# Hymba-style encoder layer: first transposes, recurrent gates, sigmoids and gelus in a new order in the two projection stages

## The chip, the cores and the metric

One NeuronCore of a Trainium2 chip runs one launch of the whole layer. The metric is device time in microseconds, the median of the runs. The engines are TensorE (PE), VectorE (DVE), ScalarE (ACT), GpSimd (POOL) and SyncE (SP, which here only issues DMAs).

## The reference, cut to what matters

The layer takes x of 4096 frames x 1024 and computes, in float32:

```
u = RMSNorm(x)
[q|k|v|x_lru|g_lru] = u @ w_in                       # 5 x 512 columns
out_A = stick-breaking attention(q, k, v)            # 8 heads x 64
xc = causal depthwise conv(4)(x_lru)
r = sigmoid(xc @ w_rgate + b_r); i = sigmoid(xc @ w_igate + b_i)   # 8 blocks x 64
a = exp(8 r log_sigmoid(lam)); u' = sqrt(1 - a^2) * i * xc
h_t = a_t h_(t-1) + u'_t                             # along the frames
out_B = h * gelu(g_lru)
h = x + concat(RMSNorm(out_A), RMSNorm(out_B)) @ w_out
h = h + HierMoE(RMSNorm(h)); y = RMSNorm(h)
```

The change touches only the projections and the recurrent branch, which are the first quarter of the time.

## The kernel before, in words

The stages run one after the other with a barrier between them: qkv, lru, attention, mix, routed experts. All engines run their own instruction lists and meet at semaphores; there is no planner, and the order on each engine is the order of the code.

The frames are cut into NG = 8 groups of GT = 512. Both projection stages handle a group in the same way (class NormedGroups). Four loads bring the group's 512 x 1024 frames; they are normalized in place (`norm`, `scale`). PE transposes one of DC = 8 chunks of 128 columns at a time into one of two PSUM banks (L217, four 128x128 transposes a chunk). ACT writes the high part of the chunk (`high`, L226), DVE the rest (`low`, L234). A product of one 128-column block is then 8 chunks x 3 matmuls of 128x512 (high x high, low x high, high x low of the weights; L243). `leading_products` makes the first two blocks' products together, chunk by chunk, with the transposes of chunk c + 2 behind the products of chunk c, so that the group starts as soon as the first chunks are split. The others follow as whole products.

The qkv stage has 12 products a group: 4 of v, 4 of q, 4 of k, in four PSUM banks. ACT copies v (L373) and DVE takes its differences along the frames, dv; PE transposes dv (L357), in two banks, between the q and the k products; ACT stages it (L381) and SP stores it. The q and k results are split by ACT (L367) and DVE (L397) and stored in pairs by SP.

The lru stage has 4 x products and 4 g products a group. ACT copies each x block (L573); DVE convolves it, one `tensor_scalar` and three `scalar_tensor_tensor` steps (L621, L625). PE then makes the gate matmuls (L565), an r and an i one for each of the 4 blocks, all in the same two banks `gate_out`, so that each pair waits until ACT's sigmoids (L580, L584) have read the pair before (`r_ready`, `i_ready`). DVE multiplies i by xc (L635). The rest of a group's work is the tail: ACT takes exp and tanh of r (L592, L594), POOL squares (L720), DVE makes the factor (L642), ACT the root (L598), POOL the input of the recurrence (L724), DVE the scan (L648) and the product with gelu(g) (L653, `out_ready`), SP the store. ACT and DVE do the tail of group G - 1 at the start of group G, behind the splits and ahead of the x copies and convolutions. The scan writes its result h into the tensor of r:

```
h = r
```

ACT's order in a group is: 8 splits, exp and tanh (4 times), 4 roots, 4 x copies, 4 gelus, 8 sigmoids. DVE's is: 8 splits, 4 factors, 4 scans, 4 products, 4 convolutions, 4 scalings of the next x, 4 products of i. Four times a group ACT loads another function table.

Of the kernel before, what the change touches and what calls it, by code (L numbers as in the profile page):

```python
# [37 lines left out]
P = 128  # L38
# [112 lines left out]
class NormedGroups:  # L151
# [161 lines left out]
def qkv(nc, k, io):  # L313

    with ExitStack() as outer:
        sb, ps, sem = alloc(nc, outer)
        weights = SplitWeights(nc, io.w_in[:, 0:3 * W_SB], 3 * W_SB, sb, sem, "qkv_")
        with ExitStack() as ctx:
# [22 lines left out]

            @block.tensor
            def _(pe):
                with pe.Fori(0, NG) as G:
                    pe.wait_ge(qk_low, G * 8 + LEAD)
                    ug.leading_products(pe, G, out[:LEAD], weights, [2 * W_SB + j * P for j in range(LEAD)], v_done)
                    for j in range(LEAD, NP):
                        pe.wait_ge(qk_low, G * 8 + j + 1)
                        ug.product(pe, G, out[j], weights, 2 * W_SB + j * P, range(DC)).then_inc(v_done, 1)
                    for j in range(NP):  # L350
                        pe.wait_ge(v_copied, G * NP + j + 1)
                        ug.product(pe, G, out[j], weights, j * P, range(DC)).then_inc(qk_done, 1)
                    for j in range(NP):
                        pe.wait_ge(dv_ready, G * NP + j + 1)
                        pe.wait_ge(dv_staged, G * NP + j + 1)
                        for b in range(TT):
                            last = nc.tensor.transpose(dv_tr[j % 2][:, b * P:(b + 1) * P],  # L357
                                                       dv[:, j, b * P:(b + 1) * P], k.ident[:])
                        last.then_inc(dv_transposed, 1)
                    for j in range(NP):  # L360
                        pe.wait_ge(qk_low, G * 8 + j + 5)
                        ug.product(pe, G, out[j], weights, W_SB + j * P, range(DC)).then_inc(qk_done, 1)
# [6 lines left out]
            def act_group(act, G, last):  # L369
# [8 lines left out]
                for j in range(NP):  # L378
                    act.wait_ge(dv_transposed, G * NP + j + NP + 1)
                    act.wait_ge(dv_stored[j % 2], G * 32 + (j // 2) * 16 + 16)  # L380
                    nc.scalar.activation(st_dv[j % 2][:], dv_tr[j % 2][:], ACT.Copy).then_inc(dv_staged, 1)  # L381
                for m in range(4, 8):
                    split_high(act, G, m)
                if not last:
                    ug.high(act, G + 1)

            @block.scalar
            def _(act):
                ug.norm(act, 0)
                first_high(act, weights, ug)  # L390
                with act.Fori(0, NG - 1) as G:
                    act_group(act, G, False)
                act_group(act, NG - 1, True)
# [6 lines left out]
            def dve_group(dve, G, last):  # L400
# [10 lines left out]
                for m in range(8):  # L411
                    split_low(dve, G, m)
                if not last:
                    ug.low(dve, G + 1)

            @block.vector
            def _(dve):
# [9 lines left out]
                with dve.Fori(0, NG - 1) as G:  # L427
                    dve_group(dve, G, False)
                dve_group(dve, NG - 1, True)
# [7 lines left out]

            def sp_group(sp, G, last):
# [4 lines left out]
                for j in range(NP):  # L443
                    hold(sp, k, dv_staged, G * NP + j + 3)
                    dst = io.dv[bass.ds(G * GT, GT), j * P:(j + 1) * P].rearrange("(b p) c -> p b c", p=P)
                    sp.dma_start(dst, st_dv[j % 2][:].rearrange("p (b c) -> p b c", b=TT)).then_inc(dv_stored[j % 2], 16)
                for m in range(4, 8):
                    store_qk(sp, G, m)
# [18 lines left out]
def lru(nc, k, io):  # L467

    with ExitStack() as outer:
# [5 lines left out]
        with ExitStack() as ctx:  # L475
# [72 lines left out]

            @block.tensor
            def _(pe):  # L550
                pe.wait_ge(gates_loaded, 64)
                with pe.Fori(0, NG) as G:
                    pe.wait_ge(g_ready, G * NL + LEAD)
                    ug.leading_products(pe, G, out[:LEAD], weights, [j * P for j in range(LEAD)], x_done)
                    for j in range(LEAD, NL):
                        pe.wait_ge(g_ready, G * NL + j + 1)
                        ug.product(pe, G, out[j], weights, j * P, range(DC)).then_inc(x_done, 1)
                    for j in range(NL):
                        pe.wait_ge(x_copied, G * NL + j + 1)
                        ug.product(pe, G, out[j], weights, W_LRU + j * P, range(DC)).then_inc(g_done, 1)  # L560
                    for j in range(NL):
                        pe.wait_ge(xc_ready, G * NL + j + 1)
                        for n, free in enumerate((r_ready, i_ready)):
                            pe.wait_ge(free, G * NL + j + 1)
                            nc.tensor.matmul(gate_out[n][:], gates[:, n, j, :], xc[:, 1, j, :],  # L565
                                             start=True, stop=True).then_inc(gate_done, 1)

            def act_middle(act, G):

                for j in range(NL):  # L570
                    act.wait_ge(x_done, G * NL + j + 1)
                    act.wait_ge(x_carried, G * NL + j + 1)
                    nc.scalar.activation(xl[:, j, H:], out[j][:], ACT.Copy).then_inc(x_copied, 1)  # L573
                for j in range(NL):
                    act.wait_ge(g_done, G * NL + j + 1)
                    act.wait_ge(out_ready, G * NL + j + 1)
                    nc.scalar.activation(gelu[:, j, :], out[j][:], ACT.Gelu_apprx_tanh).then_inc(g_ready, 1)
                for j in range(NL):
                    act.wait_ge(gate_done, G * 2 * NL + 2 * j + 1)
# [7 lines left out]
            def act_tail(act, G):  # L587

                for j in range(NL):
# [5 lines left out]
                                         scale=neg_slope[:, j:j + 1]).then_inc(th_ready, 1)  # L595
                for j in range(NL):
# [4 lines left out]
            def _(act):  # L601
# [3 lines left out]
                act_middle(act, 0)  # L605
                act.wait_ge(slope_ready, 1)
                with act.Fori(1, NG - 1) as G:
                    ug.high(act, G)
                    act_tail(act, G - 1)
                    act_middle(act, G)  # L610
                ug.high(act, NG - 1)
                act_tail(act, NG - 2)
                act_middle(act, NG - 1)
                act_tail(act, NG - 1)

            def dve_middle(dve, G, last):

                for j in range(NL):
# [12 lines left out]
                if not last:  # L631
                    ug.scale(dve, G + 1)
# [4 lines left out]
            def dve_tail(dve, G):  # L637

                for j in range(NL):
# [3 lines left out]
                                                   ALU.mult).then_inc(m2_ready, 1)  # L643
                for j in range(NL):
# [5 lines left out]
                for j in range(NL):  # L650
                    dve.wait_ge(h_ready, G * NL + j + NL + 1)
                    nc.vector.tensor_copy(state[:, j:j + 1], h[:, j, GT - 1:GT]).then_inc(state_ready, 1)
                    nc.vector.tensor_tensor(sq[:, j, :], h[:, j, :], gelu[:, j, :], ALU.mult).then_inc(out_ready, 1)  # L653

# [30 lines left out]
            def _(dve):  # L685
# [17 lines left out]
                dve_middle(dve, 0, False)  # L703
                with dve.Fori(1, NG - 1) as G:
                    ug.low(dve, G)
                    dve_tail(dve, G - 1)
                    dve_middle(dve, G, False)
                ug.low(dve, NG - 1)
                dve_tail(dve, NG - 2)
                dve_middle(dve, NG - 1, True)  # L710
                dve_tail(dve, NG - 1)
# [1200 lines left out]
```

## Time and profile before

| | us |
|---|---|
| median of 3 runs (4675.27 to 4681.49) | 4678.77 |
| the profiled execution | 4680.92 |
| its span | 4679.2 |
| PE busy | 4297.0 (92%) |
| DVE busy | 2890.4 (62%) |
| ACT busy | 2626.8 (56%) |
| POOL busy | 624.7 (13%) |
| last matmul of the qkv stage | 628.80 |
| first transpose of the lru stage | 648.81 |
| last product of the lru stage | 1147.61 |
| first matmul of attention | 1159.13 |

A "busy" of PE counts the time in which a matmul is under way; matmuls are pipelined, so those that follow each other start closer together than they last. The times below are counted from the start of the span. A row of the timeline gives start, duration, engine, line, operation, what is written and read, the shape, and how many instructions are merged; in brackets how long the engine had stood idle and who released it.

### The profile page before, as it was taken

The numbers are of one execution on the slowest core, as the hardware profiler recorded it, in microseconds if no ns is written. First come the engines' busy times: TensorE is split into PE (matmuls) and PEld (weight loads), VectorE is DVE, ScalarE is ACT, GpSimd is POOL, SyncE is SP. The second block draws the span as 40 slices with busy tenths as digits, with TensorE's granted clock in tenths as the row PEclk, the third lists the DMA queues.
The fourth block names the chain that finished last, engine by engine and source line by source line (L and its number), as shares of the span: only waits on it lengthen the run. The fifth ranks groups of instructions, "written<-read, shape, count | busy, mean of one in ns | idle before, by whom it ended". The sixth has DMA issues, their size and how long they took to land. (4 is left out here: it accounts for less than half of the span.)

```text
span 4679.2 us, 85540 instructions
## 1 busy us (share of the span) xinstructions
PE 4297.0 (92%) x28495; PEld 3209.4 (69%) x28497; DVE 2890.4 (62%) x3384; ACT 2626.8 (56%) x3994; POOL 624.7 (13%) x771
## 2 busy tenths in 40 slices
PE   7999979996998998999996999939999999999997
PEld 5878767774555555555554888827787878888776
DVE  3222236665998998999995333384655555555565
ACT  3222224444887887888885323215666666666665
POOL 0000001111000000000000000022323233232332
PEclk9999999998999999999998999969999999999999
DMA  4222231111101002011003433234666655555663
GB/s 135 94 102 102 79 119 54 54 54 65 64 29 63 22 29 70 15 39 52 6 6 105 144 126 142 101 117 166 238 222 220 213 194 190 204 192 189 220 241 139
DMA packets 279571, 539.95 MB, mean 115 GB/s; under 512 B 38320, under 2 KB 103856, under 8 KB 279344
## 3 DMA queue, kind: packets, MB, share of 16 engines
q1 hardware_dynamic: 228512, 410.49, 25.1%
q0 software_dynamic: 46224, 118.03, 7.4%
q10 hardware_dynamic: 4608, 8.39, 0.5%
q8 instruction: 144, 2.36, 0.2%
q14 instruction: 83, 0.68, 0.0%
HBM read 410.97 MB, written 176.16 MB: 125 GB/s over the span
## 5 line engine op out<-in xcount | busy, mean ns | idle before, releaser
L945 DVE TENSOR_TENSOR_SCAN att_R<-att_stay,att_R 128x512 f32<-128x512 f32 x896 | 1058.8, 1259 | 26.6 <-ACT att_stay L885 24.4
L895 ACT ACTIVATE att_RT<-att_rt 128x512 f32<-128x512 f32 (+3 forms) x1152 | 585.9, 562 | 234.3 <-PE att_rt L836 205.3
L836 PEld LDWEIGHTS att_rt<-ident,att_R 64*128 64x128 f32 x8448 | 319.9, 139 | 371.9 <-issue 368.3
L885 ACT ACTIVATE att_stay<-att_z 128x1024 f32<-128x1024 f32 (+2 forms) x576 | 554.4, 963 | 25.2 <-PE att_z L823 23.7
L849 PE MATMUL att_out<-att_RT,att_dv 128*64 128x512 f32 (+3 forms) x2304 | 522.9, 575 | 0.0
L836 PE MATMUL att_rt<-ident,att_R 64*128 64x64 f32 x8448 | 384.0, 227 | 98.0 <-ACT att_RT L895 53.2
L1257 DVE TENSOR_TENSOR ew_lo<-ew_raw,ew_hi 128x1024 fp32r<-128x1024 f32 x372 | 430.3, 1220 | 10.1 <-ACT ew_hi L1250 10.1
L1250 ACT ACTIVATE ew_hi<-ew_raw 128x1024 fp32r<-128x1024 f32 x384 | 373.7, 1050 | 0.0
L243 PE MATMUL qkv_out<-qkv_u_hi,qkv_w_hi 128*128 128x512 f32 x768 | 308.7, 402 | 16.6 <-DVE qkv_u_lo L234 16.6
L243 PE MATMUL qkv_out<-qkv_u_hi,qkv_w_lo 128*128 128x512 f32 x768 | 303.3, 395 | 0.0
L243 PE MATMUL qkv_out<-qkv_u_lo,qkv_w_hi 128*128 128x512 f32 x768 | 301.9, 393 | 0.0
L1738 ACT ACTIVATE ex_junk<-ex_y 128x1024 f32<-128x1024 f32 x80 | 84.8, 1060 | 366.0 <-DVE ex_y L1786 281.8
L1064 POOL TENSOR_TENSOR mix_sq<-mix_sq 128x512 f32<-128x512 f32 x32 | 41.9, 1308 | 1830.6 <-ACT mix_sq L1129 1830.6
L815 PE MATMUL att_z<-att_k_hi,att_q_hi 64*128 64x512 f32 (+3 forms) x1152 | 250.5, 420 | 32.7 <-DMA att_q_lo<-s_q_lo 31.6
L849 PEld LDWEIGHTS att_out<-att_RT,att_dv 128*64 128x64 f32 x2304 | 142.3, 137 | 172.8 <-issue 146.0
L397 DVE TENSOR_TENSOR qkv_st_lo<-qkv_out,qkv_st_hi 128x512 fp32r<-128x512 f32 x64 | 44.3, 692 | 325.1 <-ACT qkv_st_hi L367 325.1
L945 DVE TENSOR_TENSOR_SCAN att_R<-att_stay 128x128 f32<-128x128 f32 (+3 forms) x256 | 192.5, 805 | 77.6 <-ACT att_stay L885 73.9
L1106 PE MATMUL mix_out<-mix_w_hi,mix_hi 128*128 128x512 f32 x512 | 219.5, 429 | 11.9 <-issue 7.8
L815 PE MATMUL att_z<-att_k_lo,att_q_hi 64*128 64x512 f32 (+3 forms) x1152 | 228.1, 381 | 0.0
L815 PE MATMUL att_z<-att_k_hi,att_q_lo 64*128 64x512 f32 (+3 forms) x1152 | 227.2, 380 | 0.0
L243 PE MATMUL lru_out<-lru_u_hi,lru_w_hi 128*128 128x512 f32 x512 | 208.7, 408 | 15.3 <-DVE lru_u_lo L234 15.3
L1106 PE MATMUL mix_out<-mix_w_hi,mix_lo 128*128 128x512 f32 x512 | 214.3, 419 | 0.0
(263 smaller groups left out, 8396.2 us busy)
## 6 DMA issues: line engine op xcount, KB each, us to landing
ew_raw<-in_w_e_gate SPq DMA_DIRECT2D x32, 2048.0 KB, 9.6
ew_raw<-in_w_e_up SPq DMA_DIRECT2D x32, 2048.0 KB, 10.4
ew_raw<-in_w_e_down SPq DMA_DIRECT2D x32, 2048.0 KB, 10.0
qkv_x<-in_x SPq DMA_DIRECT2D x32, 512.0 KB, 5.3
lru_x<-in_x SPq DMA_DIRECT2D x32, 512.0 KB, 5.3
mix_raw<-s_mix_t SPq DMA_DIRECT2D x32, 512.0 KB, 4.0
mix_x<-in_x SPq DMA_DIRECT2D x32, 512.0 KB, 4.8
s_h<-mix_h SPq DMA_DIRECT2D x32, 512.0 KB, 3.5
```

The lines of the kernel that those rows point to most:

```text
L243: last = nc.tensor.matmul(bank[:], w[:, c, col:col + P], u[:, c, :], start=(c == 0 and n == 0), stop=(c == DC - 1 and n == 2))
L397: nc.vector.tensor_tensor(st_lo[m % 4][:], out[m % 4][:], f32(st_hi[m % 4][:]), ALU.subtract).then_inc(qk_low, 1)
L815: last = nc.tensor.matmul(z[t % 2][:, h * GT:h * GT + width], a[lanes, rows], b[lanes, keys], start=(n == 0), stop=(n == 2 and c != G))
L836: last = nc.tensor.transpose(rt[half][:, h, qt, :], R[lanes, n % 3, h, qt, s * P:(s + 1) * P], k.ident[lanes, lanes])
L849: last = nc.tensor.matmul(out[bank_of(G)][h * HD:(h + 1) * HD, queries], dv[:, c * TT + s, h * HD:(h + 1) * HD], RT[:, h, s].rearrange("p ...
L885: done = nc.scalar.activation(pair(stay[:, step % 4, :]), pair(z[step % 2][:]), ACT.Sigmoid, scale=-scale)
L895: nc.scalar.activation(RT[:, :, s, first:, half, :], rt[half][:, :, first:, :], ACT.Copy).then_inc(rt_copied[half], 1)
L945: nc.vector.tensor_tensor_scan(R[:, n % 3, h, s, 0:width][:, ::-1], src[:, ::-1], src[:, ::-1], initial, ALU.mult, ALU.bypass).then_inc(sc ...
L1106: end = nc.tensor.matmul(half_out[half][n][:], a[:, t, c, :], w[:, c, n * GT:(n + 1) * GT], start=(c == half * NP and m == 0), stop=(c == ...
L1250: self.nc.scalar.activation(self.hi[:, m, cols], self.raw[:, m, cols], ACT.Copy).then_inc(self.high_ready[m], 1)
L1257: engine.tensor_tensor(self.lo[:, m, cols], self.raw[:, m, cols], f32(self.hi[:, m, cols]), ALU.subtract).then_inc(self.low_ready[m], 1)
L1738: nc.scalar.activation(junk[:], y[:], ACT.Square, accum_out=total[:]).then_inc(squared, 1)
```

## The change

Nothing is computed otherwise; instructions change their places.

Both stages: the transposes of chunks 0 and 1 (`first_transposes`) leave `leading_products`. They stand ahead of the loop for group 0 and in the middle of the last product of group G for group G + 1. ACT and DVE split these two chunks at the end of group G, ahead of the last split of k (qkv) or the last gelu (lru), and the other six at the start of group G + 1.

qkv stage: PE transposes dv block j - 1 behind q product j, and the last behind the first k product. ACT's copies and SP's stores of dv are interleaved with those of q and k accordingly.

lru stage, PE: gates of block 0 behind g product 0, of block 1 between the halves of product 1, of block 2 behind product 1, of block 3 between the halves of product 2. ACT: splits, x copies 0 and 1, exp and tanh of group G - 1, x copy 2, roots of G - 1, x copy 3, sigmoids, gelus 0 to 2, the first two splits of G + 1, gelu 3. The r sigmoid gets the wait for `out_ready`. DVE: splits, convolutions 0 and 1, factors of G - 1, convolutions 2 and 3, scans and products of G - 1 (these now also wait for `g_ready`), scaling of the next x, products of i. POOL is as it was.

```diff
-    def leading_products(self, pe, G, banks, weights, cols, done):
+    def first_transposes(self, pe, G):
 
         self.transpose(pe, G, 0)
         self.transpose(pe, G, 1)
+
+    def leading_products(self, pe, G, banks, weights, cols, done):
+
         for c in range(DC):
...
+            def pe_group(pe, G, last):
...
+                for j in range(NP):
+                    pe.wait_ge(v_copied, G * NP + j + 1)
+                    ug.product(pe, G, out[j], weights, j * P, range(DC)).then_inc(qk_done, 1)
+                    if j > 0:
+                        pe_dv(pe, G, j - 1)
+                for j in range(NP):
+                    pe.wait_ge(qk_low, G * 8 + j + 5)
+                    if j < NP - 1:
+                        ug.product(pe, G, out[j], weights, W_SB + j * P, range(DC)).then_inc(qk_done, 1)
+                    else:
+                        ug.product(pe, G, out[j], weights, W_SB + j * P, range(DC // 2))
+                        if not last:
+                            ug.first_transposes(pe, G + 1)
+                        ug.product(pe, G, out[j], weights, W_SB + j * P, range(DC // 2, DC)).then_inc(qk_done, 1)
+                    if j == 0:
+                        pe_dv(pe, G, NP - 1)
...
+            def act_group(act, G, first, last):
+                if not first:
+                    ug.high(act, G, range(2, DC))
...
-                for m in range(4):
+                for m in range(7):
                     split_high(act, G, m)
...
+                    if 0 < m <= NP:
+                        stage_dv(act, G, m - 1)
                 if not last:
-                    ug.high(act, G + 1)
+                    ug.high(act, G + 1, range(2))
+                split_high(act, G, 7)
...
-                for m in range(4):
+                for m in range(8):
                     store_qk(sp, G, m)
...
+                    if 0 < m <= NP:
+                        store_dv(sp, G, m - 1)
...
+            def pe_gates(pe, G, j):
+                pe.wait_ge(xc_ready, G * NL + j + 1)
+                for n, free in enumerate((r_ready, i_ready)):
+                    pe.wait_ge(free, G * NL + j + 1)
+                    nc.tensor.matmul(gate_out[n][:], gates[:, n, j, :], xc[:, 1, j, :],
+                                     start=True, stop=True).then_inc(gate_done, 1)
...
+                for j in range(NL):
+                    pe.wait_ge(x_copied, G * NL + j + 1)
+                    ug.product(pe, G, out[j], weights, W_LRU + j * P, range(DC // 2))
+                    if j in (1, 2):
+                        pe_gates(pe, G, 2 * j - 1)
+                    if j == NL - 1 and not last:
+                        ug.first_transposes(pe, G + 1)
+                    ug.product(pe, G, out[j], weights, W_LRU + j * P, range(DC // 2, DC)).then_inc(g_done, 1)
+                    if j in (0, 1):
+                        pe_gates(pe, G, 2 * j)
...
+            def sigmoids(act, G):
+
                 for j in range(NL):
                     act.wait_ge(gate_done, G * 2 * NL + 2 * j + 1)
+                    act.wait_ge(out_ready, G * NL + j + 1)
                     nc.scalar.activation(r[:, j, :], gate_out[0][:], ACT.Sigmoid,
                                          bias=k.b_r[:, j:j + 1]).then_inc(r_ready, 1)
...
+                if not first:
+                    ug.high(act, G, range(2, DC))
+                for j in (0, 1):
+                    copy_x(act, G, j)
+                if not first:
+                    decays(act, G - 1)
+                copy_x(act, G, 2)
+                if not first:
+                    roots(act, G - 1)
+                copy_x(act, G, 3)
+                sigmoids(act, G)
+                if first:
+                    act.wait_ge(slope_ready, 1)
+                if last:
+                    decays(act, G)
+                    roots(act, G)
+                    for j in range(NL):
+                        gelu_of(act, G, j)
+                else:
+                    for j in range(NL - 1):
+                        gelu_of(act, G, j)
+                    ug.high(act, G + 1, range(2))
+                    gelu_of(act, G, NL - 1)
...
+            def dve_group(dve, G, first, last):
+
+                if not first:
+                    ug.low(dve, G, range(2, DC))
+                convolve(dve, G, (0, 1))
+                if not first:
+                    factors(dve, G - 1)
+                convolve(dve, G, (2, 3))
+                if not first:
+                    recurrence(dve, G - 1)
+                if not last:
+                    ug.scale(dve, G + 1)
+                gated_inputs(dve, G)
+                if not last:
+                    ug.low(dve, G + 1, range(2))
```

## Rows read from the trace of the kernel before

**Rows 1.** Windows by stage: length, busy us (instructions) of each engine, clock, DMA, GB/s.

```profile
111.50:555.10 443.60, 432.83 (x2018) 353.49 (x2017) 106.23 (x198) 116.29 (x198) 0.00 (x0) 1.00 0.27 99
714.70:1068.40 353.70, 338.41 (x1442) 251.29 (x1441) 231.93 (x312) 164.94 (x241) 70.06 (x48) 1.00 0.14 53
```

**Rows 2.** Timeline at the seam between qkv groups 0 and 1.

```profile
111.77 1.03 PE L217 MATMUL qkv_tr<-ident,qkv_x 128*128 128x128 f32 x8
...
112.46 1.26 ACT L226 ACTIVATE qkv_u_hi<-qkv_tr,g_norm 128x512 fp32r<-128x512 f32 x2
...
114.00 0.50 PE L243 MATMUL qkv_out<-qkv_u_hi,qkv_w_hi 128*128 128x512 f32 x1 [1.20 <-DVE qkv_u_lo L234]
```

**Rows 3.** Timeline of PE, second half of the dv transposes, qkv group 0.

```profile
88.84 1.11 PE L357 MATMUL qkv_dv_tr<-ident,qkv_dv 128*128 128x128 f32 x8 [0.42 <-ACT qkv_st_dv L381]
```

**Rows 4.** Timeline of PE at the seam between lru groups 4 and 5.

```profile
941.83 1.88 PE L565 MATMUL lru_gate_out<-lru_xc,lru_gates 128*128 128x512 f32 x4
944.77 5.89 PE L565 MATMUL lru_gate_out<-lru_xc,lru_gates 128*128 128x512 f32 x12 [1.06 <-ACT lru_r L580]
950.49 1.04 PE L217 MATMUL lru_tr<-ident,lru_x 128*128 128x128 f32 x8
952.82 0.50 PE L243 MATMUL lru_out<-lru_u_hi,lru_w_hi 128*128 128x512 f32 x1 [1.29 <-DVE lru_u_lo L234]
```

**Rows 5.** Timeline of ACT and DVE, last input sigmoid and last product of the stage.

```profile
1127.53 0.69 ACT L584 ACTIVATE lru_ig<-lru_gate_out,b_i 128x512 f32<-128x512 f32 x1 [0.17 <-PE lru_gate_out L565]
...
1147.61 0.68 DVE L653 TENSOR_TENSOR lru_sq<-lru_r,lru_gelu 128x512 f32<-128x512 f32 x1
```

**Rows 6.** Timeline of PE, lru group 4: first and last leading matmul, first of the g products.

```profile
893.88 0.50 PE L243 MATMUL lru_out<-lru_u_hi,lru_w_hi 128*128 128x512 f32 x1 [1.30 <-DVE lru_u_lo L234]
...
908.00 0.40 PE L243 MATMUL lru_out<-lru_u_hi,lru_w_lo 128*128 128x512 f32 x1
...
919.43 0.39 PE L243 MATMUL lru_out<-lru_u_hi,lru_w_hi 128*128 128x512 f32 x1
```

**Rows 7.** Groups by line, lru seams 714.7 to 1068.4: busy us, mean ns, idle before.

```profile
L565 PE MATMUL lru_gate_out<-lru_xc,lru_gates 128*128 128x512 f32 x97 | 47.0, 606 | 6.5 <-ACT lru_r L580 6.4
```

**Rows 8.** Timeline of POOL and DVE, narrow windows, tail of lru group 3.

```profile
909.23 1.04 POOL L720 TENSOR_TENSOR lru_sq<-lru_a 128x512 f32<-128x512 f32 x1
909.24 1.58 DVE L642 SCALAR_TENSOR_TENSOR lru_th<-lru_sq,lru_th 128x512 f32<-128x512 f32 x1 [2.57 <-POOL lru_sq L720]
...
913.63 0.68 DVE L642 SCALAR_TENSOR_TENSOR lru_th<-lru_sq,lru_th 128x512 f32<-128x512 f32 x1
...
915.58 1.30 POOL L724 TENSOR_TENSOR lru_sq<-lru_th,lru_ig 128x512 f32<-128x512 f32 x1
...
915.66 2.31 DVE L648 TENSOR_TENSOR_SCAN lru_r<-lru_a,lru_state,lru_sq 128x512 f32<-128x512 f32 x1 [1.34 <-POOL lru_sq L724]
...
922.23 1.25 DVE L648 TENSOR_TENSOR_SCAN lru_r<-lru_a,lru_state,lru_sq 128x512 f32<-128x512 f32 x1
```

**Rows 9.** Timeline of ACT and DVE behind these scans: table load and first convolution.

```profile
924.20 1.28 ACT L577 ACT_TABLE_LOAD   x1 [3.97 <-DVE lru_sq L653]
...
926.03 0.53 DVE L621 TENSOR_SCALAR lru_xc<-lru_xl,conv_w,conv_b 128x512 f32<-128x512 f32 x1
926.60 2.33 DVE L625 SCALAR_TENSOR_TENSOR lru_xc<-lru_xl,conv_w,lru_xc 128x512 f32<-128x512 f32 x3
...
929.14 0.55 DVE L621 TENSOR_SCALAR lru_xc<-lru_xl,conv_w,conv_b 128x512 f32<-128x512 f32 x1
```

**Rows 10.** Windows between the qkv and lru stages, columns as in the first group.

```profile
628.00:630.00 2.00, 1.20 (x6) 0.64 (x4) 0.13 (x1) 0.60 (x1) 0.00 (x0) 1.00 0.00 0
...
634.00:636.00 2.00, 0.00 (x0) 0.00 (x0) 0.98 (x2) 1.07 (x1) 0.95 (x1) 0.52 0.00 0
...
648.00:650.00 2.00, 1.19 (x6) 1.20 (x7) 1.81 (x3) 0.09 (x2) 0.00 (x0) 0.50 0.00 0
...
654.00:656.00 2.00, 2.00 (x11) 1.57 (x10) 1.47 (x2) 1.00 (x2) 0.00 (x0) 0.86 0.67 242
```

More of the change, by code:

```diff
@@ L340, in qkv, with pe_dv @@
             block = ctx.enter_context(nc.Block())
+            def pe_dv(pe, G, j):
+                pe.wait_ge(dv_ready, G * NP + j + 1)
+                pe.wait_ge(dv_staged, G * NP + j + 1)
+                for b in range(TT):
+                    last = nc.tensor.transpose(dv_tr[j % 2][:, b * P:(b + 1) * P],
+                                               dv[:, j, b * P:(b + 1) * P], k.ident[:])
+                last.then_inc(dv_transposed, 1)
+            def pe_group(pe, G, last):
+                pe.wait_ge(qk_low, G * 8 + LEAD)
+                ug.leading_products(pe, G, out[:LEAD], weights, [2 * W_SB + j * P for j in range(LEAD)], v_done)
+                for j in range(LEAD, NP):
+                    pe.wait_ge(qk_low, G * 8 + j + 1)
+                    ug.product(pe, G, out[j], weights, 2 * W_SB + j * P, range(DC)).then_inc(v_done, 1)
+                for j in range(NP):
[14 more added lines that the diff above has]
+                        pe_dv(pe, G, NP - 1)
@@ L342, in _ @@
             @block.tensor
             def _(pe):
[L344 to L362, printed above, removed]
@@ L364, in split_high @@
+                ug.first_transposes(pe, 0)
+                with pe.Fori(0, NG - 1) as G:
+                    pe_group(pe, G, False)
+                pe_group(pe, NG - 1, True)
             def split_high(act, G, m):
@@ L551, in _, with copy_x @@
                 pe.wait_ge(gates_loaded, 64)
[L552 to L577, printed above, removed]
+                ug.first_transposes(pe, 0)
+                with pe.Fori(0, NG - 1) as G:
+                    pe_group(pe, G, False)
+                pe_group(pe, NG - 1, True)
+            def copy_x(act, G, j):
+                act.wait_ge(x_done, G * NL + j + 1)
+                act.wait_ge(x_carried, G * NL + j + 1)
+                nc.scalar.activation(xl[:, j, H:], out[j][:], ACT.Copy).then_inc(x_copied, 1)
+            def sigmoids(act, G):
                 for j in range(NL):
                     act.wait_ge(gate_done, G * 2 * NL + 2 * j + 1)
+                    act.wait_ge(out_ready, G * NL + j + 1)
                     nc.scalar.activation(r[:, j, :], gate_out[0][:], ACT.Sigmoid,
@@ L585, in act_middle, with gelu_of, act_group, decays @@
                                          bias=k.b_i[:, j:j + 1]).then_inc(i_ready, 1)
-            def act_tail(act, G):
+            def gelu_of(act, G, j):
+                act.wait_ge(g_done, G * NL + j + 1)
+                act.wait_ge(out_ready, G * NL + j + 1)
+                nc.scalar.activation(gelu[:, j, :], out[j][:], ACT.Gelu_apprx_tanh).then_inc(g_ready, 1)
+            def act_group(act, G, first, last):
+                if not first:
[21 more added lines that the diff above has]
+                    gelu_of(act, G, NL - 1)
+            def decays(act, G):
                 for j in range(NL):
@@ L604, in _, with convolve @@
                 first_high(act, weights, ug)
-                act_middle(act, 0)
-                act.wait_ge(slope_ready, 1)
+                act_group(act, 0, True, False)
                 with act.Fori(1, NG - 1) as G:
[L608 to L618, printed above, removed]
+                    act_group(act, G, False, False)
+                act_group(act, NG - 1, False, True)
+            def convolve(dve, G, blocks):
+                for j in blocks:
                     dve.wait_ge(x_copied, G * NL + j + 1)
@@ L702, in _ @@
                 first_low(dve, weights, ug)
-                dve_middle(dve, 0, False)
+                dve_group(dve, 0, True, False)
                 with dve.Fori(1, NG - 1) as G:
[L705 to L711, printed above, removed]
+                    dve_group(dve, G, False, False)
+                dve_group(dve, NG - 1, False, True)
+                factors(dve, NG - 1)
+                recurrence(dve, NG - 1)
             @block.gpsimd
```

58 lines of the change are left out of this document (33 added, 25 removed).

## The prediction

> **What bounds the kernel now.** I read the windows by stage first, to see how much of the projection time the tensor engine leaves free, then the timelines at the seams between groups, to see which wait ends last there, and then VectorE (DVE), ScalarE (ACT) and GpSimd (POOL) inside one group. TensorE (PE) sets the time of both projection stages: over the six middle seams of the qkv stage it is busy 432.8 of 443.6 us, over those of the lru stage 338.4 of 353.7, while DVE has 231.9 and ACT 164.9 there [rows 1]. The holes in PE are few and sit at the same places in each group. At a qkv seam the eight first transposes are issued over 0.9 us, and PE then stands 1.20 us until the first chunk is split by ACT and DVE [rows 2]. In the middle of a qkv group the second half of the dv transposes waits 0.42 us for ACT [rows 3]. At an lru seam the gate matmuls stretch over 8.66 us, because the sigmoids must empty two banks between them, and then come 2.33 us for the first transposes, in 1.29 of which PE stands [rows 4]. After the last lru group there is a tail without PE: from the last input sigmoid to the end of the last product it takes 20.8 us [rows 5], and attention starts behind it.
>
> **The change part by part. The qkv stage.** The first transposes move into the last product, so what follows them (two ACT splits from 112.46 on, two DVE splits behind them [rows 2]) runs under the half product behind them: 12 matmuls of 0.23, 2.8 us (four products of 24 take 22.4, from 919.43 to 941.83 [rows 4, 6]). The first split starts about 0.6 us after its transposes and the two pairs take some 2.2 us, so the cover is thin, but the first product needs only the first pair. Were it gone, the old 1.20 us would come back. Saved per seam: 2.23 less 0.9 for the transposes themselves, plus 0.1 for the slow first matmul after a stall (busy 0.50 where others take 0.40 [rows 2, 6]): 1.4 us, times 7 seams = 9.8. The dv transposes go one block at a time behind products, so that the 0.42 us and 0.1 for the restart go: times 8 groups = 4.2 [rows 3]. The dv copies on ACT and the dv stores in SP's queue move along, between the q and k stores, in the order in which their data become ready; each buffer has two products' time before it is used again, so I cost both at nothing. qkv: -14.0 us.
>
> **The lru stage, what it removes.** The seam gives 1.4 us as above. The 16 gate matmuls alone need 16 x 0.43 = 6.9 us (four are busy 1.88, of which the last one 0.6), so 1.8 of the 8.66 goes [rows 4, 7]. That is 3.2 us per group: the 58.94 us from seam to seam (893.88 to 952.82 [rows 4, 6]) would become 55.7. The number of table loads stays four a group, since exp and tanh, sqrt, sigmoid and gelu are still in four blocks.
>
> **What it adds: a wait in front of the second gates.** The gates of block 1 now stand in the middle of the second g product, and all gates share two banks. So PE waits there for the first r sigmoid of this group (r_ready), and behind that wait stand two and a half g products, the other gates and the next group's transposes. The sigmoid itself now waits for out_ready of the group before, because r and h are one tensor. And out_ready comes from the recurrence, which DVE now does after all four convolutions. Before, the recurrence came first and the gates last, so the two never met. I time this chain from T = 0, the first leading matmul of a group, with the offsets of the group at 893.88.
>
> PE arrives: first g product at 919.43, T = 25.5 [rows 6]; a product 5.6, gates 1.7, half a product 2.8: T = 35.6.
>
> DVE starts its first convolution when block 0 is copied: the last leading matmul is at 908.00 [rows 6], that of block 0 0.7 earlier, then 0.4 to land and 0.6 for the copy: T = 14.4. Then in its new order: four convolutions of 3.11 (926.03 to 929.14) = 12.4; four factors of 0.68 = 2.7; four scans of 1.25 = 5.0; the first product 0.7 [rows 5, 8, 9]. 20.8 us, T = 35.2. This is the least it can be.
>
> POOL runs inside this stretch: four squares and four products of the previous group. Where such a pair meets in the trace, the DVE instruction is stretched: a factor takes 1.58 beside a square and 0.68 alone, a scan 2.31 beside a product and 1.25 alone [rows 8]. A meeting costs DVE 0.9 to 1.1. Before, no convolution met a POOL instruction, so for it the price is not shown; bounds are nothing (its steps take 0.78 alone [rows 9]) and the same price. Its three steps are the same operation as the factor (L625, L642: two SBUF tensors in, one out), so I take the price of the factor. The squares can only start after the decays, which now come behind the first x copies (T = 17), the products after the factors and roots (T = 24), so all eight fall where DVE has no gap: 8 x 0.95 = 7.6, T = 42.8. The Trainium skill, page "SBUF — State Buffer", section "Who interferes with whom", says that a DVE instruction with two SBUF inputs contends with a GpSimd instruction that reads SBUF, and that the loser blocks for the whole of it. By that rule the convolutions pay too, and the eight meetings cost the whole POOL time, the upper bound below. The trace agrees where it shows a meeting [rows 8].
>
> Then ACT: in the trace the gelu's table load waited for out_ready and started as soon as it was there [rows 9]. The sigmoid has its two waits in the same order now, so its load, 1.28, and the sigmoid, 0.69 [rows 5, 9], come behind out_ready: T = 44.8. PE's stall is 44.8 - 35.6 = 9.2 us in each group from 1 to 7. Group 0 has no recurrence before it.
>
> **The clock.** The last qkv matmuls ran at 629, and in the window from 634 on the granted clock is 0.52, so it fell at the window's beginning, 5 us after the work ended. It was 0.50 when PE resumed at 648.8 and 0.86 over 654 to 656, so it rose at about 654.6 [rows 10]. A stall of 9 us is longer than those 5, so I expect the 1.2 GHz level after it, for up to the 5.8 us seen there: at half speed that costs 0 to 2.9, and I take 2.1, as gates and products follow without a gap. Together X = 11.3 us per stalled group. Bounds: low, 0.7 per meeting and no fall of the clock, X = 7.2; high, POOL's time as it is, 4 x 1.04 + 4 x 1.30 = 9.4 instead of 7.6, and the clock at 2.9, X = 13.9.
>
> **The tail.** In the last group the gates come before the last products, so the 20.8 us chain would start earlier, but X delays it. The last input sigmoid now starts at T = 44.8 + three gate pairs 5.1 + two halves 5.6 + clock 2.1 = 57.6 and 0.2 to land; before, at 1127.53 [rows 5], T = 56.8 (that group's T = 0 is 952.82 + 2 x 58.94 = 1070.7). So +1.0. The gelus stand behind the roots on ACT but are done before DVE's last scan: nothing.
>
> **Sum.** Groups 1 to 6: 6 x (X - 3.2); group 0: -3.2; group 7: X - 10.3. lru = 7X - 32.7 = +46.4 with X = 11.3. With qkv, -14.0: 7X - 46.7 = **+32 us**. The profiled execution took 4680.92 us, 1.7 more than its span and 2.1 above the median of 4678.77; against the median the forecast is 4711. The change pays only below X = 6.7. Attention and the later stages only shift.
>
> **Rivals.** (1) *Faster: convolutions don't contend with POOL.* Only factors and scans would pay: X = 35.2 + 1 + 1.28 + 0.69 - 35.6 = 2.6, too short for the clock. 7 x 2.6 - 46.7 = -28, 4650 us. For: no row shows such a meeting. Against: the same operation pays [rows 8]. It decides at X = 6.7. (2) *The change does what its moves say and nothing waits,* X = 0: -47 us, 4632. Against: DVE's bare sum ends at 35.2, with load and sigmoid still behind it, and PE arrives at 35.6. (3) *The stall is there, but the clock isn't lost:* X = 9.2, +18 us, 4696. (4) *It is worse:* in turns with POOL the roots and the fourth x copy come late too, or the slow level lasts through the following gates: X = 14 to 16, +51 to +65, 4730 to 4744.
>
> **How the numbers follow.** Forecast 0.60, (1) 0.12, (2) 0.03, (3) 0.13, (4) 0.12. The range takes in (3), most of (4) and the bounds of X (7.2 gives 4682, 13.9 gives 4729), and leaves out (1), (2) and the end of (4): 4682 to 4738. About 0.2%, 9 us, is what this measurement can tell from no change. Slower 0.83; same 0.04, for X between 5.4 and 8; faster 0.13.
>
> **What would show it.** In the changed profile: no PE idle on qkv_u_lo at the qkv seams, none on the dv copies, a qkv stage 14 us shorter. In lru groups 1 to 7 one PE idle of about 9 us in front of gate matmuls, released by ACT's lru_r; convolution steps of about 1.7 us beside POOL instead of 0.78; a period of about 67 us, with the clock at 0.50 for some us after the stall; in group 0 no stall. I am wrong if the stall is under 6 us, if the convolution steps stay at 0.78 beside POOL, or if the clock stays at 1.00.

## The result, and the profile after

| | before | after |
|---|---|---|
| median, us (6 runs each) | 4678.82 (4675.27 to 4682.34) | 4702.40 (4697.66 to 4703.12) |
| ratio, with its 95% interval | | 1.0047 (1.0036 to 1.0057) |
| span of the profiled execution | 4679.2 | 4701.3 |
| last matmul of the qkv stage | 628.80 | 613.25 |
| first transpose of the lru stage | 648.81 | 633.23 |
| first matmul of attention | 1159.13 | 1179.76 |

The changed kernel is slower by 23.6 us, where +32 was forecast. The two profiled executions differ by 22.1, and the table splits this: the qkv stage ends 15.6 us earlier (forecast 14.0), the lru stage from its first transpose to attention takes 546.5 us instead of 510.3, 36.2 more (forecast 46.4), and the rest of the span is 1.5 us longer. The rest is the same code in both kernels. In the profiled executions of the kernels below it takes 3519.9 to 3527.8 us (one kernel that works on other numbers left out), so 1.5 is within what it varies by.

The windows of the changed kernel for the qkv seams, with the columns of [rows 1]:

```profile
108.40:551.80 443.40, 442.38 (x2082) 362.97 (x2082) 111.87 (x205) 120.77 (x206) 0.00 (x0) 1.00 0.28 101
```

PE is now busy 442.38 of 443.40 us, where it had 432.83 of 443.60. The timeline of its PE, where the seam wait of [rows 2] and the dv wait of [rows 3] were:

```profile
93.28 0.60 PE L349 MATMUL qkv_dv_tr<-ident,qkv_dv 128*128 128x128 f32 x4
107.47 1.04 PE L217 MATMUL qkv_tr<-ident,qkv_x 128*128 128x128 f32 x8
...
123.79 0.50 PE L243 MATMUL qkv_out<-qkv_u_hi,qkv_w_hi 128*128 128x512 f32 x1 [0.17 <-DVE qkv_u_lo L234]
...
179.29 1.03 PE L217 MATMUL qkv_tr<-ident,qkv_x 128*128 128x128 f32 x8
```

Neither transpose row has a bracket, so nothing stood before them. The only wait left in a qkv group is 0.17 us ahead of its last leading chunk. From 107.47 to 179.29 a group takes 71.8 us.

The lru stage, timeline of PE for group 4, to compare with [rows 4, 6]:

```profile
826.06 1.04 PE L217 MATMUL lru_tr<-ident,lru_x 128*128 128x128 f32 x8
...
865.05 0.39 PE L243 MATMUL lru_out<-lru_u_hi,lru_w_lo 128*128 128x512 f32 x1
873.13 2.04 PE L582 MATMUL lru_gate_out<-lru_xc,lru_gates 128*128 128x512 f32 x2 [7.69 <-ACT lru_r L620]
...
891.22 1.04 PE L217 MATMUL lru_tr<-ident,lru_x 128*128 128x128 f32 x8
```

At the seam no wait is left, but in the middle of the second g product PE stands 7.69 us for the first r sigmoid, exactly in front of the gates of block 1. The same stall is in groups 1 to 7 (7.69 five times, 8.10 once, 7.47 in the last; mean 7.72), and not in group 0. Over 700 to 1130 us the groups by line sum it up: all the idle time of PE in front of gates has the one releaser (columns as in [rows 7]).

```profile
L582 PE MATMUL lru_gate_out<-lru_xc,lru_gates 128*128 128x512 f32 x100 | 57.8, 708 | 46.6 <-ACT lru_r L620 46.6
```

What the stall waits for is read backwards. The timeline of ACT:

```profile
871.00 1.28 ACT L620 ACT_TABLE_LOAD   x1 [13.26 <-DVE lru_sq L726]
872.30 0.69 ACT L620 ACTIVATE lru_r<-lru_gate_out,b_r 128x512 f32<-128x512 f32 x1
```

ACT has been idle for 13.26 us; the table load of the sigmoid itself starts only when DVE's product is there. The timeline of DVE for the same group, in narrow windows so that rows are not merged:

```profile
844.09 0.55 DVE L689 TENSOR_SCALAR lru_xc<-lru_xl,conv_w,conv_b 128x512 f32<-128x512 f32 x1 [1.69 <-ACT lru_xl L613]
844.68 0.75 DVE L693 SCALAR_TENSOR_TENSOR lru_xc<-lru_xl,conv_w,lru_xc 128x512 f32<-128x512 f32 x1
...
847.22 1.17 DVE L689 TENSOR_SCALAR lru_xc<-lru_xl,conv_w,conv_b 128x512 f32<-128x512 f32 x1
848.43 1.41 DVE L693 SCALAR_TENSOR_TENSOR lru_xc<-lru_xl,conv_w,lru_xc 128x512 f32<-128x512 f32 x1
...
852.98 0.69 DVE L711 SCALAR_TENSOR_TENSOR lru_th<-lru_sq,lru_th 128x512 f32<-128x512 f32 x1
...
854.80 1.79 DVE L711 SCALAR_TENSOR_TENSOR lru_th<-lru_sq,lru_th 128x512 f32<-128x512 f32 x1
856.51 1.51 DVE L689 TENSOR_SCALAR lru_xc<-lru_xl,conv_w,conv_b 128x512 f32<-128x512 f32 x1
858.06 1.66 DVE L693 SCALAR_TENSOR_TENSOR lru_xc<-lru_xl,conv_w,lru_xc 128x512 f32<-128x512 f32 x1
859.76 1.67 DVE L693 SCALAR_TENSOR_TENSOR lru_xc<-lru_xl,conv_w,lru_xc 128x512 f32<-128x512 f32 x1
861.46 0.75 DVE L693 SCALAR_TENSOR_TENSOR lru_xc<-lru_xl,conv_w,lru_xc 128x512 f32<-128x512 f32 x1
...
865.47 1.28 DVE L720 TENSOR_TENSOR_SCAN lru_r<-lru_a,lru_state,lru_sq 128x512 f32<-128x512 f32 x1
...
870.24 0.68 DVE L726 TENSOR_TENSOR lru_sq<-lru_r,lru_gelu 128x512 f32<-128x512 f32 x1
```

and POOL beside it:

```profile
848.11 1.18 POOL L806 TENSOR_TENSOR lru_sq<-lru_a 128x512 f32<-128x512 f32 x1
849.34 1.40 POOL L806 TENSOR_TENSOR lru_sq<-lru_a 128x512 f32<-128x512 f32 x1
...
857.70 1.47 POOL L810 TENSOR_TENSOR lru_sq<-lru_th,lru_ig 128x512 f32<-128x512 f32 x1
859.13 1.75 POOL L810 TENSOR_TENSOR lru_sq<-lru_th,lru_ig 128x512 f32<-128x512 f32 x1
```

A convolution step takes 0.75 us alone, 1.41 beside a square and 1.66 beside a product; the second convolution (847.22 to 852.98, 5.76 us) costs 2.6 more than the first (3.13), the third (5.91) 2.8 more, the fourth factor 1.1. Eight DVE instructions met the eight of POOL, for 6.5 us in all. DVE has no gap between 844.09 and the end of the product at 870.92.

The granted clock through this stall, each window asked for by itself, columns as in [rows 1]:

```profile
867.00:869.00 2.00, 0.00 (x0) 0.00 (x0) 2.00 (x2) 0.00 (x0) 0.00 (x0) 1.00 0.00 0
...
869.00:871.00 2.00, 0.00 (x0) 0.00 (x0) 2.00 (x6) 0.00 (x0) 0.00 (x0) 0.67 0.00 0
...
873.00:875.00 2.00, 1.87 (x3) 0.87 (x4) 2.00 (x4) 0.56 (x1) 0.00 (x0) 0.50 0.88 341
...
875.00:877.00 2.00, 2.00 (x5) 0.99 (x4) 1.16 (x2) 0.89 (x2) 0.00 (x0) 0.62 0.00 0
...
877.00:879.00 2.00, 2.00 (x10) 1.59 (x10) 0.69 (x1) 0.49 (x1) 0.00 (x0) 1.00 0.00 0
```

PE stopped at about 865.4. A share of 0.67 over 869 to 871 puts the fall to 1.2 GHz at about 869.7, 4.3 us after that, and 0.62 over 875 to 877 puts the rise at about 876.5. The first gate matmuls after the stall therefore run at half speed (two are busy 2.04 us at 873.13, where four take 1.88 [rows 4]). Over the seven stalls the work done at the low level lasted 3.1 to 5.9 us, 4.2 in the mean, of which half is lost: an estimate of 2.1 us a stall.

### The profile page after: what moved, and what is told of

Read it like the earlier page. It is cut to its first block and busy times, and to the rows that moved or that the text cites. A ratio compares the mean times of both kernels' runs of the same rounds, so it can differ in the third digit from the quotient of the medians.

```text
span 4701.3 us, 85463 instructions
## 1 busy us (share of the span) xinstructions
PE 4295.1 (91%) x28496; PEld 3210.2 (68%) x28497; DVE 2896.7 (62%) x3384; ACT 2627.3 (56%) x3994; POOL 623.4 (13%) x771
## 5 line engine op out<-in xcount | busy, mean ns | idle before, releaser
L1343 DVE TENSOR_TENSOR ew_lo<-ew_raw,ew_hi 128x1024 fp32r<-128x1024 f32 x372 | 430.1, 1218 | 10.1 <-ACT ew_hi L1336 10.1
L243 PE MATMUL lru_out<-lru_u_hi,lru_w_hi 128*128 128x512 f32 x512 | 225.4, 440 | 5.5 <-DVE lru_u_lo L234 5.5
```

Source lines behind the costliest of these rows:

```text
L243: last = nc.tensor.matmul(bank[:], w[:, c, col:col + P], u[:, c, :], start=(c == 0 and n == 0), stop=(c == DC - 1 and n == 2))
L1343: engine.tensor_tensor(self.lo[:, m, cols], self.raw[:, m, cols], f32(self.hi[:, m, cols]), ALU.subtract).then_inc(self.low_ready[m], 1)
```

## Experiments

All of them start from the changed kernel. Each comparison is against the kernel before, run again beside them: 4682.30 us for the lru part alone, the same memory with the wait, less contention and the later gates, 4681.79 for the other four. Where two kernels are compared, it is by their differences from these. PE times are of each run's own profile.

**The two stages apart.** The first kernel has only the qkv part of the change, the second only the lru part.

```diff
 # qkv part alone: lru() is that of the kernel before, with
+                    ug.first_transposes(pe, G)
                     ug.leading_products(pe, G, out...
 # lru part alone: the same in qkv(), and lru() as changed
```

> Only the qkv stage of the change; the lru stage is that of before. My theory: the two parts don't touch each other, and the qkv part is a gain of 15 us (its last matmul moved from 628.80 to 613.25), so about 4664 against 4679, faster by 0.3%. Rival: the gain of the qkv stage is given back behind it (barrier, first loads of the lru stage), and the total is within 5 us of before.

> Only the lru stage of the change; the qkv stage is that of before. My theory: the two parts add up, and the lru part alone costs 36 us (its stage was longer by that much in the changed kernel): about 4715 to 4718. Rival: the parts influence each other, and the sum of the two parts' differences is off from the 22 us of both by more than 6 us.

Measured: qkv part alone 4669.75 (6 runs), ratio 0.9970 (0.9958 to 0.9983), 12 us faster, where 15 was expected. In its profile the stage ends at 615.95, 2.7 us later than in the whole change with the same code, and the difference is there at the first seam already (110.42 instead of 107.47): the first group's time varies by that much. Its seams and gates in the lru stage are as before (1.06 us in front of the second block's gates). Lru part alone 4716.54 (4 runs), ratio 1.0071 (1.0054 to 1.0088), 34 us slower, with the 7.69 us stall in its place. The two sum to +22, against +23.6 for the change: within the intervals the parts add up, and the whole loss is in the lru part.

**The wait taken away.** h gets a tensor of its own, so the sigmoid needs no `out_ready`. To make room, the scratch tensor `junk` is no longer set aside where the projections don't use it.

```diff
-        self.junk = sb(tag + "junk", [P, D])
+        self.junk = None if normed else sb(tag + "junk", [P, D])
...
-            h = r
+            h = sb("lru_h", [P, NL, GT])
...
                     act.wait_ge(gate_done, G * 2 * NL + 2 * j + 1)
-                    act.wait_ge(out_ready, G * NL + j + 1)
```

> The whole change, but the scan writes h into a tensor of its own (it takes the place of a scratch tensor that the lru stage never uses), and the r sigmoid no longer waits for out_ready. My theory: this wait is the only source of the stall in front of the gates of block 1. Without it X = 0: no PE idle before the gate matmuls, period 55.7 us in the lru stage, the clock at 1.00 through the groups, and 7X - 46.7 gives about -47 us: 4630. Rival 1: DVE and POOL are the bound after all, and the stall moves to the gates of blocks 2 and 3 (waiting for xc_ready) or to the seam: 4650 to 4680. Rival 2: the ACT order (sigmoids behind the roots and the fourth x copy) holds the first sigmoid anyway: some us of stall stay in each group.

Measured: 4636.33 (4 runs), ratio 0.9903 (0.9887 to 0.9918), 45.5 us faster than the kernel before. The timeline of its PE, group 4, and the start of attention:

```profile
842.14 1.88 PE L582 MATMUL lru_gate_out<-lru_xc,lru_gates 128*128 128x512 f32 x4
846.65 1.88 PE L582 MATMUL lru_gate_out<-lru_xc,lru_gates 128*128 128x512 f32 x4
851.16 1.88 PE L582 MATMUL lru_gate_out<-lru_xc,lru_gates 128*128 128x512 f32 x4
855.67 1.88 PE L582 MATMUL lru_gate_out<-lru_xc,lru_gates 128*128 128x512 f32 x4
...
1111.89 0.48 PE L900 MATMUL att_z<-att_k_hi,att_q_hi 64*128 64x128 f32 x2 [23.50 <-DMA att_q_lo<-s_q_lo]
```

Four gate pairs, none with a bracket. The group takes 55.57 us (from the transposes at 807.42 to those at 862.99) where the prediction's own working without a stall said 55.7, and attention starts 47.2 us earlier than before, where the sum with X = 0 says 46.7. Everything that the change removes is really removed; the wait alone turns it round.

With the wait something else goes too. The timeline of ACT in this kernel:

```profile
839.13 1.28 ACT L619 ACT_TABLE_LOAD   x1
843.19 0.69 ACT L619 ACTIVATE lru_r<-lru_gate_out,b_r 128x512 f32<-128x512 f32 x1 [2.78 <-PE lru_gate_out L582]
```

Here the table load is done 2.78 us before its sigmoid can start. In the changed kernel it came behind the last wait, so 1.28 of the 7.69 us are the load.

**The same memory, with the wait.** As above, but the wait is back.

```diff
             h = sb("lru_h", [P, NL, GT])
...
+                    act.wait_ge(out_ready, G * NL + j + 1)
```

> The whole change with h in a tensor of its own, but the r sigmoid still waits for out_ready: the control for the run without the wait. My theory: the place of h costs and gives nothing, the stall is 7.7 us again, 4702. Rival: moving h in memory was part of the gain: under 4690.

Measured in one run: 4702.33, a stall of 7.69 us in the same place, attention at 1178.19. That is 20 us slower than before, against 45.5 faster without the wait. So it was the wait, and not where h or the scratch tensor lies.

**DVE's order.** The recurrence of group G - 1 ahead of convolutions 2 and 3, everything else as changed.

```diff
-                convolve(dve, G, (2, 3))
                 if not first:
                     recurrence(dve, G - 1)
+                convolve(dve, G, (2, 3))
```

> The whole change, but DVE does the scans and products of group G - 1 ahead of convolutions 2 and 3 instead of behind them. My theory: the stall comes from the place of the recurrence in DVE's order. Two convolutions, about 8.8 us with their meetings with POOL, leave the chain, but DVE now waits for POOL's last inputs and the scans meet POOL, so that the stall falls from 7.7 to 2 to 4 us, mostly too short for the clock; the total is 20 to 30 us under before, 4650 to 4660. Rival (the meetings alone are the cause): DVE's and POOL's sum in front of out_ready is the same in either order, the stall stays above 6 us and the total near 4700.

Measured: 4651.07 (4 runs), ratio 0.9936 (0.9921 to 0.9952), 31 us faster than before. The timeline of its PE:

```profile
851.29 1.96 PE L582 MATMUL lru_gate_out<-lru_xc,lru_gates 128*128 128x512 f32 x4 [1.72 <-ACT lru_r L620]
```

The stall shrinks from 7.69 to 1.72 us with the same wait still there and the same instructions; the gates behind it run at full speed (1.96 us for four), and the group takes 57.5 us. `out_ready` was late because two convolutions stood in front of the recurrence. The scans now meet POOL (2.32 us, 2.25 and 2.22 for the first three, where 1.26 to 1.28 is their time in the changed kernel), so the eight meetings are still in the chain: the order is what counts.

**The clock.** 30 extra matmuls per stalled group, written to a bank that is free at that moment, in front of the wait. The result is the same; the first group is written out by itself, since it has no stall.

```diff
+                    if j == 1 and not first:
+                        pe.wait_ge(x_copied, G * NL + NL)
+                        for _ in range(WARM):
+                            nc.tensor.matmul(out[3][:], weights.hi[:, 0, 0:P], ug.hi[:, 0, :], start=True, stop=True)
                     if j in (1, 2):
                         pe_gates(pe, G, 2 * j - 1)
```

> The whole change, with 30 extra matmuls in front of the gates of block 1 in groups 1 to 7, into a bank that is free then (its content isn't used), about 7 us of work in the 7.7 us in which PE stands. My theory: the stall stays in length, but the granted clock doesn't fall, and the matmuls behind the stall are at 0.23 us instead of 0.43: about 2.2 us per group, 15 in all: 4687. Rival: the slow matmuls behind the stall don't come from the clock, or the clock counts other work and falls anyway: 4702 or slower.

Measured: 4693.49 (10 runs), ratio 1.0025 (1.0015 to 1.0034). The timeline of its PE:

```profile
871.70 1.95 PE L583 MATMUL lru_gate_out<-lru_xc,lru_gates 128*128 128x512 f32 x4 [0.69 <-ACT lru_r L626]
```

The sigmoid comes no earlier (the gates start 47.1 us after the group's transposes in both kernels), but the clock stays at 1.00 and the four gates take 1.95 us. The group takes 63.50 us in the mean instead of 65.66: the clock's share of X is 2.16 us, and seven times that is 15 of the change's loss. The lru stage is 13.8 us shorter; attention starts at 1168.74, only 11 us earlier, because the qkv stage ended 2.8 us later in this execution. By the medians the kernel is 11.7 us slower than before, where the change was 23.6. The other 7.7 us of X are plain waiting.

**Less contention.** POOL's squares become a write of a constant, and its two waits go through `hold`, which adds the increment of a counter to each; this kernel leaves out the squares, so its recurrence has other inputs.

```diff
-                        pool.wait_ge(a_ready, G * NL + j + 1)
-                        pool.wait_ge(stored[j], G * 16 + 16)
-                        nc.gpsimd.tensor_tensor(sq[:, j, :], a[:, j, :], a[:, j, :], ALU.mult).then_inc(sq_ready, 1)
+                        hold(pool, k, a_ready, G * NL + j + 1)
+                        hold(pool, k, stored[j], G * 16 + 16)
+                        nc.gpsimd.memset(sq[:, j, :], 0.5).then_inc(sq_ready, 1)
```

> The whole change, but POOL writes a constant in place of each of the four squares of a group (so the recurrence's inputs are wrong), a memset that reads nothing from SBUF. My theory, with the rule that a DVE instruction with two SBUF inputs contends with a GpSimd instruction that reads SBUF: the three convolution steps beside them take 0.75 each instead of 1.41, R0 comes 2.6 us earlier, and the stall falls from 7.7 to about 5. Rival: any POOL instruction blocks them, reading or not, for its own length: steps stay above 1.1 and the stall above 6.5.

Measured in one run: 4671.64, attention at 1163.92, a stall of 5.12 us. Timelines of its DVE and POOL, and of its PE:

```profile
842.67 0.73 DVE L689 TENSOR_SCALAR lru_xc<-lru_xl,conv_w,conv_b 128x512 f32<-128x512 f32 x1
843.44 2.33 DVE L693 SCALAR_TENSOR_TENSOR lru_xc<-lru_xl,conv_w,lru_xc 128x512 f32<-128x512 f32 x3
...
843.73 0.53 POOL L806 MEMSET lru_sq<- 128x512 f32 x1 [0.61 <-ACT lru_a L663]
...
866.01 3.75 PE L582 MATMUL lru_gate_out<-lru_xc,lru_gates 128*128 128x512 f32 x4 [5.12 <-ACT lru_r L620]
```

Three convolution steps beside a POOL instruction that reads nothing take 2.33 us, exactly as alone [rows 9]; beside the squares three took 4.3. The stall is 2.57 us shorter, and 0.62 + 3 x 0.66 = 2.6 is what the squares had added to the second convolution. So the contention is in the stall nearly one for one. The clock fell in these stalls too (four gates take 3.75 us). The total is not a measure of the contention: attention starts 15.8 us earlier than in the changed kernel, but another 15.5 us are saved behind attention's start, where this kernel works on other numbers. That part was not traced.

**Gates one product later.** Each pair of gates one g product behind its place in the change, the wait kept.

```diff
-                    if j in (1, 2):
-                        pe_gates(pe, G, 2 * j - 1)
+                    if j in (2, 3):
+                        pe_gates(pe, G, 2 * j - 3)
...
-                    if j in (0, 1):
-                        pe_gates(pe, G, 2 * j)
+                    if j in (1, 2):
+                        pe_gates(pe, G, 2 * j - 2)
```

> The whole change with each pair of gates one product later: block 0 behind g product 1, block 1 in the middle of product 2, block 2 behind it, block 3 in the middle of product 3. Nothing else differs. My theory: the r sigmoid of block 0 is ready at the same time after the group's start as in the changed kernel, PE arrives 5.6 us later, and the 7.7 us of stall fall to about 2, too short for the clock; the last sigmoids, gelus and first splits then come late at the seam, 1 to 2 us. X of 3 to 4 instead of 10: 4652 to 4662. Rival: the stall moves along with the gates (the sigmoid waits for something that the gates themselves start): it stays at 6 to 8 us, 4690 to 4710.

Measured: 4676.69 (10 runs), ratio 0.9987 (0.9977 to 0.9997), 5.6 us faster than before and less than expected of it. The timeline of its PE, and the clock:

```profile
863.98 3.37 PE L582 MATMUL lru_gate_out<-lru_xc,lru_gates 128*128 128x512 f32 x4 [2.08 <-ACT lru_r L620]
...
881.65 0.50 PE L243 MATMUL lru_out<-lru_u_hi,lru_w_hi 128*128 128x512 f32 x1 [1.35 <-DVE lru_u_lo L234]
...
1151.61 0.48 PE L901 MATMUL att_z<-att_k_hi,att_q_hi 64*128 64x128 f32 x2 [29.28 <-DMA att_q_lo<-s_q_lo]
```

```profile
862.00:864.00 2.00, 0.02 (x1) 0.05 (x1) 2.00 (x6) 1.99 (x3) 0.00 (x0) 1.00 0.55 209
864.00:866.00 2.00, 2.00 (x3) 0.93 (x4) 2.00 (x4) 0.73 (x2) 0.00 (x0) 0.59 0.83 315
866.00:868.00 2.00, 2.00 (x5) 1.06 (x4) 1.02 (x2) 0.98 (x2) 0.00 (x0) 0.55 0.00 0
```

The stall came out at the size expected, 2.1 us. Three things had been left out. The clock falls in five of the seven groups although PE stood for only 2.1 us; in the group shown the share of 0.59 puts the fall at about 864.4, when the gates had just begun. ACT reaches the splits of the next group later: its sigmoids end at 877.4, then come a table load and three gelus, and the splits of the transposes issued at 876.47 start at 880.11 (0.6 us behind them in the changed kernel), so a seam wait like that of the kernel before is back (1.35 us). And with the gates nearer to the end of the last group, PE stands 29.28 us ahead of attention instead of 22.91. Such a group takes 61.15 us, 5.6 more than without the wait.

## Why the prediction was right, and where its sizes were off

The side, the place and the mechanism were as forecast: one stall per group, in groups 1 to 7 alone, in front of the gates of block 1, released by the r sigmoid, whose wait ends with the recurrence. That the wait is the cause is shown by the two kernels with h in its own tensor: with the wait +20 us, without it -45.5. By the terms:

- **qkv, -14.0; measured -15.6.** Both waits went as worked out. The group became 2.1 us shorter, where 1.4 + 0.5 had been put down. The 1.6 us more should not be read closely: the same qkv code ended at 615.95 in the kernel that has it alone, which would be -12.9, for its first group took longer.
- **lru without the stall, 55.7 us a group; measured 55.57** in the kernel without the wait.
- **PE arrives at T = 35.6; measured 35.7.** T = 0 of group 4 is 829.7 (826.06, the transposes, half a product), and PE stops at 865.44.
- **DVE starts at T = 14.4; measured 14.4** (844.09).
- **DVE's bare sum 20.8; measured 20.3.** Factors and scans that follow each other start 0.60 and 1.19 us apart, less than their busy times of 0.68 and 1.25 by which I counted.
- **Eight meetings, 7.6; measured 6.5.** The number was right; a meeting costs a convolution step 0.66 beside a square and 0.9 beside a product, not the 0.95 taken from the factor. With this, `out_ready` came at T = 41.2 instead of 42.8.
- **Table load and sigmoid, 2.0; measured 2.2** with the landing at PE. Sum: a stall of 7.7 instead of 9.2. The sizes of the DVE terms carry nearly all of the miss.
- **The tail, +1.0 at X = 11.3.** The last input sigmoid was forecast at T = 57.6; with X smaller by 1.4 that is 56.2, and it is at 56.2 (1148.50, group 7's T = 0 at 1092.3). From there to the end of the last product it is 20.8 us as before (1169.28 less 1148.50).
- **Clock, 2.1; measured 2.16** by the kernel with extra matmuls, 2.1 estimated from the windows. The size was right, the reasoning only in part: the clock fell 2.5 to 5.3 us into the stall, before the 5 us in six of seven, and in the kernel with late gates it was lost around a stall of 2.1 us. Rival (3), that the clock isn't lost, was less likely than I thought, and "too short for the clock" in rival (1) would not have been safe.
- **The sum.** With X = 7.7 + 2.2 = 9.9 (10.1 by the groups' times, 65.66 less 55.57) the formula gives 7 x 9.9 - 32.7 = +36.6 for lru, measured +36.2, and 7 x 9.9 - 46.7 = +22.6 in all, measured +22.1 between the profiled executions. The forecast of +32.4 was 10.3 too high against these: 10.2 in lru, of which seven times the 1.4 by which X was too large are 9.8, and 1.6 in qkv, less 1.5 behind attention's start. The medians differ by 23.6, so the total comes 1.5 nearer to the forecast than its terms do, and that is luck.

The total alone would not have decided for the forecast: rival (3), the stall without the loss of the clock, had 4696, and 4702.40 is nearer to that than to 4711. The windows decide, since the clock fell in each of the seven stalls. Rival (4) did not come about: ACT's fourth x copy ended at 857.74, 7.7 us before PE stopped, and X stayed below 14. Of the other rivals, (1), that convolutions don't contend, is ruled out by the steps of 1.41 and 1.66 us, and by their return to 0.78 when POOL's squares read nothing. Here the trace agrees with the Trainium skill, page "SBUF — State Buffer", section "Who interferes with whom", that the two-input DVE form and a GpSimd instruction reading SBUF contend. The steps did not, however, pay the whole POOL time as the upper bound of the forecast had it: 0.66 for a square of 1.18 to 1.49. Rival (2), no stall, needs the wait gone, as the kernel with its own h shows. What stays open: why the clock fell at the 2.1 us stall of the late gates in groups 2 to 6 and not in group 1, whose stall was as long (2.10), nor in group 7 (1.88), and which of the r sigmoid's two waits holds back the table load; no run swaps them.

## What to carry to other kernels

When work that used to stand at the end of a group is moved to its middle, ask first whose buffer it writes: here `h = r` turned a sigmoid's output into a wait on the previous group's recurrence, and one tensor of 8 KB a partition (an unused scratch tensor gave 4 KB of it) made the same reordering 1% faster instead of 0.5% slower. If the tensor can't be had, put the producer of the releasing semaphore ahead of independent work on its engine: two convolutions behind the recurrence instead of ahead of it were worth 54 us. Price a wait by a timeline from one T = 0 on both sides of it; and when a forecast depends on how far two engines overlap, count what one takes in the other's company.

## What the runs showed of the hardware that was not expected

- A `tensor_scalar` (one tensor input) beside a reading POOL instruction is stretched too: 1.17 us beside a square and 1.51 beside a product, 0.55 alone. Beside POOL's write of a constant it took 0.73, while the two-input steps there kept their 0.78.
- The granted clock fell in the middle of stalls of 7.7 us, 2.5 to 5.3 us after the last matmul, while an idle of 1.72 us in every group left it at 1.00, and one of 2.1 us was followed by some 3.4 us at 1.2 GHz in five of the six groups that had it.
- ACT's table load did not start in 13 us of idle time in front of a sigmoid with two waits, `gate_done` and `out_ready` (871.00), so its 1.28 us were paid after the wait. With `gate_done` alone it ran ahead of the wait (839.13, the sigmoid 2.78 us after its end). Whether a load can run under a wait is to be read from the trace: no run here changes the number or the order of the waits and nothing else.
